# A hybrid decoder layer on one core: the head's norm weights spread by TensorE, x loaded ahead of the weights, first weight tiles in row halves

## The chip, the cores and the metric

The kernel runs on one core of one Trainium2 chip. The metric is the device time of one execution in microseconds (us). The profile shown is of one execution; start times in it count from the start of its span.

## What is computed

One layer over x (256 tokens, 1024 features, fp32): half a SwiGLU FFN, a mixer (block-sparse attention beside a state-space part, one output projection), half a second FFN, and a final norm. The stretch that matters here is the start:

```python
def rms_norm(x, w):
    y = xf * lax.rsqrt(jnp.mean(xf * xf, axis=-1, keepdims=True) + EPS)
    return y * w

def swiglu(h, w1, w3, w2):
    return (jax.nn.silu(h @ w1) * (h @ w3)) @ w2

h = rms_norm(x, ffn1_norm)                     # x 256 x 1024
x = x + 0.5 * swiglu(h, ffn1_w1, ffn1_w3, ffn1_w2)   # w1, w3 1024 x 2816, w2 2816 x 1024
```

## The kernel before

Every engine's program is written out by hand in `build`, with semaphores between them; no scheduler orders anything. Tokens are in two tiles of 128 (`t` = 0, 1), features in 8 tiles of 128 (`KD`). A matrix product in fp32 is made of three products of parts in fp32r (`three`, L1099; lines 1101 to 1103): an operand is split into a high part, copied by ScalarE (`w_hi`, `hT_hi`), and a low part, the difference, made by VectorE (`w_lo`, `hT_lo`).

The first FFN takes its 22 column tiles of w1 and w3 in 11 steps of two (`odd` = 0, 1). Step 0 is laid out by tokens: `pair_product(n, t, odd)` (L1148) multiplies the transposed, normed tile `t` with tile `odd` of w1 and w3 together, 8 feature tiles by three matmuls of 256 columns. From step 1 on `gate_or_up` makes the transposed result with the weights stationary.

The head, until step 1, runs as follows. The tiles are named by (odd, kind), kind 0 for w1, 1 for w3, 2 for w2.

- SP (L297 to L317) issues: x of token tile 0 in two halves, the identity (part of `cst`), the norm's weights broadcast to all 128 partitions (`norm_w`, 512 KB written), w1 and w3 of tile 0 (512 KB each), x of token tile 1, w1 and w3 of tile 1, both w2 tiles, the other constants. Then each load of step 1 (`ffn_load`, L275, 1 MB) waits until the split of the tile before it in that buffer is done (`half_ready`).
- ScalarE squares x with a sum (`square_x`, L476); POOL makes `rstd` from it (`rsqrt`, L363 and L366).
- VectorE scales x with `rstd` and the norm's weights (`scale_first`, L792), in halves of 512 features.
- TensorE multiplies the identity with itself without a use for the result (`keep_clock`, L1172; the fillers, in U_BANK), transposes the normed tile (`norm_transposes`, L1230), and ScalarE and VectorE split the transposes (`hT_hi_part`, L488; `hT_lo_part`, L813).
- ScalarE and VectorE split the weight tiles (`split_hi`, L452; `split_lo`, L770), 1024 elements per partition each.

TensorE's order is its program in `ffn`: five fillers, transposes of token tile 0, eleven fillers, product (t 0, odd 0), transposes of token tile 1, products (0, 1), (1, 0), (1, 1), then the gate product of step 1, `pair_transposes` and its up product. Each engine's instructions wait in the order in which they are written, so an instruction that waits holds all behind it.

Of the kernel before, what the change touches and what calls it, by code (L numbers as in the profile page):

```python
# [37 lines left out]
PAIR_ORDER = ((0, 0), (0, 1), (1, 0), (1, 1), (0, 2), (1, 2))  # L38
# [43 lines left out]
def build(nc, x_in, w1s, w3s, w2s, norms, w_in, conv_w, conv_b, dt_bias, A_log, D_skip,  # L82
# [4 lines left out]
    with ExitStack() as ctx:  # L87
# [29 lines left out]

        gu = sb("gu", [P, SEQ])
# [43 lines left out]
        first_loaded = [sem(f"first_loaded{k}") for k in range(3)]  # L162
        consts_loaded = sem("consts_loaded")
# [96 lines left out]

        def mix_half(m):
# [34 lines left out]
        def _(sp):  # L296
# [8 lines left out]
            sp.dma_start(norm_w[:, 0, :], norms[0].partition_broadcast(P)).then_inc(norm_loaded[0], 16)  # L305

            for odd, kind in PAIR_ORDER:
                if (odd, kind) == (1, 0):
                    load_x(1, 0)
                    load_x(1, 1)  # L310
# [35 lines left out]
        def _(pool):  # L346
# [6 lines left out]

            step(pool.memset(minus_half[:, :], -0.5))
# [44 lines left out]
            for t in range(TT):  # L399
                rsqrt(2 * t + 2, t, D)  # L400

# [45 lines left out]
        def _(act):  # L447
# [11 lines left out]
            def first_hi(kind):  # L459
                _, slot, src = ffn_half(0, 0, 0, kind)  # L460
                split_hi(slot, src, first_loaded[kind], 16, kind < 2)

# [87 lines left out]
            first_hi(0)  # L550
            norm_hi(0, 0)
            first_hi(1)
            for c in range(2):
                act.wait_ge(x_loaded[2 + c], 16)
                square_x(0, 1, c)
            ffn_hi(0, 0, 1, 0)
            ffn_hi(0, 0, 1, 1)
            norm_hi(0, 1)
# [196 lines left out]
        def _(dve):  # L755
# [29 lines left out]
            def scale_first(t):  # L785

                if t == 0:
                    dve.wait_ge(norm_loaded[0], 16)
                dve.wait_ge(rstd_ready, t + 1)
                for c, done in enumerate((scaled_left, scaled_right)):  # L790
                    cols = slice(c * 512, (c + 1) * 512)
                    dve.scalar_tensor_tensor(normed[:, t, cols], x[:, t, cols], rstd[:, t:t + 1], norm_w[:, 0, cols],  # L792
                                             ALU.mult, ALU.mult).then_inc(done, 1)

# [303 lines left out]
        def _(pe):  # L1098
# [49 lines left out]
            def pair_product(n, t, odd):  # L1148
# [26 lines left out]

# [422 lines left out]
```

## Time and profile before

| | us |
|---|---|
| median of 3 runs | 576.69 (575.89 to 576.89) |
| the profiled execution, whole | 575.76 |
| its span | 574.0 |
| TensorE matmul busy | 557.4 (97% of the span) |
| VectorE busy | 324.3 (56%) |
| ScalarE busy | 288.8 (50%) |
| POOL busy | 49.3 (9%) |

A busy time is the sum over the engine's instructions. In the rows below, PE is TensorE's matmul side, DVE VectorE, ACT ScalarE, SP the engine that issues the large loads. `128x512 x2` is an instruction form and how often it stands there; a bracket behind a row names what ended the idle time ahead of it. An fp32 matmul of the program (128x128, the fillers) shows as two rows.

### The profile page before, as it was taken

How to read it: one execution, taken by the hardware profiler on the slowest of the kernel's cores; microseconds unless marked ns; L12 is line 12 of the kernel's file. 1: busy time of each engine (PE TensorE's matmuls, PEld its weight loads, DVE VectorE, ACT ScalarE, POOL GpSimd, SP SyncE). 2: the span in 40 equal slices, each digit the busy share in tenths (PEclk: the TensorE clock that was granted, in tenths of full speed). 3: DMA queues.
4: the chain of work that ended last, by engine and by line, in shares of the span. 5: the costliest groups of instructions: out<-in, count | busy, mean ns of one | idle time of the engine just before them, and what ended most of it. 6: DMA issues, size and time to landing. Idle time of an engine off the chain costs nothing.

```text
span 574.0 us, 9569 instructions
## 1 busy us (share of the span) xinstructions
PE 557.4 (97%) x3744; PEld 511.4 (89%) x3744; DVE 324.3 (56%) x434; ACT 288.8 (50%) x463; POOL 49.3 (9%) x86
## 2 busy tenths in 40 slices
PE   5999999999999999999999999999999999999994
PEld 5999999999999979998888788789999999999993
DVE  3654554545554584877676546575545554554544
ACT  4644443444344375867666755364443444453433
POOL 1000040000000020513340102010000000000001
PEclk9999999999999999999999999999999999999998
DMA  9845497655446737556323226353566655456701
GB/s 256 313 128 200 154 288 247 219 164 188 155 157 213 242 117 210 175 175 199 113 91 113 73 75 186 107 152 121 174 215 219 193 173 165 151 196 219 219 1 74
DMA packets 69448, 98.01 MB, mean 171 GB/s; under 512 B 1828, under 2 KB 55392, under 8 KB 69424
## 3 DMA queue, kind: packets, MB, share of 16 engines
q1 hardware_dynamic: 68576, 95.21, 51.6%
q0 software_dynamic: 848, 2.47, 1.6%
q8 instruction: 16, 0.26, 0.2%
q14 instruction: 8, 0.07, 0.0%
HBM read 96.62 MB, written 1.05 MB: 170 GB/s over the span
## 4 chain that ended last, share of the span: by engine, by line
PE 92%; DVE 3%; ACT 2%; DMA 1%; POOL 1%; issue 1%; SPq 0%; POOLq 0%; DVEq 0%; ACTq 0%
PE bank L1101 28%; PE bank L1102 28%; PE bank L1103 28%; DMA raw<-in_ffn_w 1%; PE bank L1230 1%; DVE w_lo L770 1%; ACT z_silu L476 1%; PE bank L1404 1%; POOL mean_sq L363 1%; DVE x L782 1%; PE bank L1403 1%; PE bank L1375 1%; PE bank L1376 1%; PE bank L1362 1%; PE bank L1374 0%
## 5 line engine op out<-in xcount | busy, mean ns | idle before, releaser
L770 DVE TENSOR_TENSOR w_lo<-raw,w_hi 128x1024 fp32r<-128x1024 f32 x176 | 211.1, 1228 | 148.0 <-ACT w_hi L452 147.3
L452 ACT ACTIVATE w_hi<-raw 128x1024 fp32r<-128x1024 f32 x176 | 179.6, 1054 | 112.3 <-PE bank L1103 70.7
L1101 PE MATMUL bank<-hT_hi,w_hi 128*128 128x256 f32 x736 | 208.6, 283 | 0.0
L1103 PE MATMUL bank<-hT_hi,w_lo 128*128 128x256 f32 x736 | 208.3, 283 | 0.0
L1102 PE MATMUL bank<-hT_lo,w_hi 128*128 128x256 f32 x736 | 208.2, 283 | 0.0
L1101 PEld LDWEIGHTS bank<-hT_hi,w_hi 128*128 128x128 f32 x736 | 141.1, 192 | 1.6
L1102 PEld LDWEIGHTS bank<-hT_lo,w_hi 128*128 128x128 f32 x736 | 141.1, 192 | 1.4
L1103 PEld LDWEIGHTS bank<-hT_hi,w_lo 128*128 128x128 f32 x736 | 141.1, 192 | 0.0
L1101 PE MATMUL bank<-w_hi,hT_hi 128*128 128x512 f32 (+1 forms) x192 | 69.6, 362 | 0.6 <-DVE w_lo L770 0.5
L1101 PE MATMUL bank<-w_hi,gu_hi 128*128 128x512 f32 x176 | 69.2, 393 | 0.3
L1102 PE MATMUL bank<-w_lo,gu_hi 128*128 128x512 f32 x176 | 69.0, 392 | 0.0
L1103 PE MATMUL bank<-w_hi,gu_lo 128*128 128x512 f32 x176 | 68.5, 389 | 0.0
L1103 PE MATMUL bank<-w_hi,hT_lo 128*128 128x512 f32 (+1 forms) x192 | 68.2, 355 | 0.0
L1102 PE MATMUL bank<-w_lo,hT_hi 128*128 128x512 f32 (+1 forms) x192 | 68.0, 354 | 0.0
L503 ACT ACTIVATE gu_hi<-gu 128x256 fp32r<-128x256 f32 x40 | 16.7, 419 | 88.8 <-DVE gu L827 83.1
L1101 PEld LDWEIGHTS bank<-w_hi,hT_hi 128*128 128x128 f32 x192 | 36.3, 189 | 5.7 <-DVE w_lo L770 1.3
L1103 PEld LDWEIGHTS bank<-w_hi,hT_lo 128*128 128x128 f32 x192 | 36.3, 189 | 5.3
L1102 PEld LDWEIGHTS bank<-w_lo,hT_hi 128*128 128x128 f32 x192 | 36.4, 189 | 4.3
L1103 PEld LDWEIGHTS bank<-w_hi,gu_lo 128*128 128x128 f32 x176 | 33.1, 188 | 7.2
L1101 PEld LDWEIGHTS bank<-w_hi,gu_hi 128*128 128x128 f32 x176 | 33.2, 189 | 6.9 <-issue 1.1
L1102 PEld LDWEIGHTS bank<-w_lo,gu_hi 128*128 128x128 f32 x176 | 33.2, 189 | 5.3
L363 POOL TENSOR_SCALAR mean_sq<-sumsq 128x1 f32<-128x1 f32 x8 | 4.8, 594 | 346.2 <-ACT z_silu L476 346.2
(164 smaller groups left out, 423.2 us busy)
## 6 DMA issues: line engine op xcount, KB each, us to landing
raw<-in_ffn_w SPq DMA_DIRECT2D x63, 1024.0 KB, 5.5
raw<-in_w_in SPq DMA_DIRECT2D x16, 1024.0 KB, 5.5
raw<-in_w_out SPq DMA_DIRECT2D x6, 1024.0 KB, 4.9
raw<-in_ffn_w SPq DMA_DIRECT2D x6, 512.0 KB, 7.2
x<-in_x SPq DMA_DIRECT2D x4, 256.0 KB, 4.1
out_x<-normed SPq DMA_DIRECT2D x4, 256.0 KB, 2.1
norm_w<-in_ffn_norm SPq DMA_DIRECT2D x1, 512.0 KB, 5.5
norm_w<-in_mix_norm POOLq DMA_DIRECT2D x1, 512.0 KB, 6.6
```

The costliest lines, as they stand in the source:

```text
L363: step(pool.tensor_scalar(m, sumsq[:, 0, col:col + 1], sumsq[:, 1, col:col + 1], EPS, ALU.add, ALU.add))
L452: act.activation(by_tile(dst) if columns else dst, src, ACT.Copy).then_inc(hi_ready, 1)
L476: act.activation(z_silu[:, t, cols], x[:, t, cols], ACT.Square, scale=D ** -0.5, accum_out=sumsq[:, c, r:r + 1]).then_inc(sq_ready, 1)
L503: act.activation(gu_hi[:, odd, :], gu[:, :], ACT.Copy).then_inc(gu_hi_ready, 1)
L770: dve.tensor_tensor(lo, src, hi, ALU.subtract).then_inc(half_ready, 1)
L782: dve.scalar_tensor_tensor(xs, bank[:, 2 * t + c, :], 1.0 if n == 2 else 0.5, xs, ALU.mult, ALU.add).then_inc(x_ready, 1)
L1101: pe.matmul(dst, lhs[0], rhs[0], start=start, stop=False, skip_group_check=True)
L1102: pe.matmul(dst, lhs[0], rhs[1], start=False, stop=False, skip_group_check=True)
L1103: return pe.matmul(dst, lhs[1], rhs[0], start=False, stop=stop, skip_group_check=True)
L1230: last = pe.transpose(bank[:, bank_n, k * P:(k + 1) * P], normed[:, t, col + k * P:col + (k + 1) * P], ident)
L1362: pe.matmul(b[:, 0:384], select_r[:, h:h + 1].to_broadcast([P, P]), csT[:, :], start=True, stop=False, skip_group_check=True)
L1375: pe.matmul(bank[:, 7, o], m[:, P:SEQ], x_tok[:, 0, c], start=True, stop=False)
```

## The change

- The norm's weights come as one row of 1024 numbers (4 KB) into partition 0. TensorE spreads it over the partitions by two fp32 products with a row of ones (`spread_norm`), each of 512 columns, into two PSUM banks, at the very start of its program. `scale_first` reads the weights from there. POOL sets the row of ones first.
- SP loads all of x behind that row, and only then weights. The first tiles of w1 and w3 come in halves of four feature tiles, 256 KB each: both upper halves, then both lower.
- ScalarE squares all of x first; then it takes hT_hi's halves and the upper weight halves in turn, the lower halves, hT_hi of token tile 1, and the second pair of weight tiles behind it. VectorE takes hT_lo and the upper halves in turn, scales token tile 1, and splits w3's lower half; POOL splits w1's lower half.
- TensorE: five fillers in place of eleven ahead of the first product, which now waits for the upper halves alone, and again at feature tile 4 for the lower ones. In the first FFN product (1, 0) comes before product (0, 1).

```diff
@@ SP
             sp.dma_start(cst[:, C_ID:C_ID + P], consts[:, C_ID:C_ID + P]).then_inc(ident_loaded, 16)
-            sp.dma_start(norm_w[:, 0, :], norms[0].partition_broadcast(P)).then_inc(norm_loaded[0], 16)
-
-            for odd, kind in PAIR_ORDER:
-                if (odd, kind) == (1, 0):
-                    load_x(1, 0)
-                    load_x(1, 1)
+            sp.dma_start(norm_row, norms[0].rearrange("(a d) -> a d", a=1)).then_inc(norm_loaded[0], 16)
+            load_x(1, 0)
+            load_x(1, 1)
+            for low in range(2):
+                for kind in range(2):
+                    src = (w1s, w3s)[kind][0].rearrange("(k p) f -> p k f", p=P)[:, 4 * low:4 * low + 4, 0:P]
+                    sp.dma_start(first_src(kind, low), src).then_inc((first_loaded if low else first_top_loaded)[kind], 16)
+            for odd, kind in SECOND_ORDER:
@@ POOL
+            pool.memset(ones_row, 1.0).then_inc(ones_ready, 1)
...
             for t in range(TT):
                 rsqrt(2 * t + 2, t, D)
+            _, slot, _ = ffn_half(0, 0, 0, 0)
+            pool.wait_ge(hi_ready, 1)
+            pool.tensor_tensor(first_part(w_lo[:, slot, :], 1), first_src(0, 1),
+                               first_part(w_hi[:, slot, :].bitcast(f32), 1), ALU.subtract).then_inc(first_low_ready, 1)
@@ ScalarE
+            def first_rows_hi(kind, low):
+                act.wait_ge((first_loaded if low else first_top_loaded)[kind], 16)
+                act.activation(first_part(w_hi[:, ffn_half(0, 0, 0, kind)[1], :], low), first_src(kind, low),
+                               ACT.Copy).then_inc(hi_ready if low else first_top_hi, 1)
...
                 square_x(0, 0, c)
-            first_hi(0)
-            norm_hi(0, 0)
-            first_hi(1)
             for c in range(2):
                 act.wait_ge(x_loaded[2 + c], 16)
                 square_x(0, 1, c)
+            hT_hi_part(hT_count(0) + 1, T_BANKS[0], 0, 0)
+            first_rows_hi(0, 0)
+            hT_hi_part(hT_count(0) + 2, T_BANKS[1], 4, 0)
+            first_rows_hi(1, 0)
+            first_rows_hi(0, 1)
+            first_rows_hi(1, 1)
+            norm_hi(0, 1)
             ffn_hi(0, 0, 1, 0)
             ffn_hi(0, 0, 1, 1)
-            norm_hi(0, 1)
             first_hi(2)
@@ VectorE
-                if t == 0:
-                    dve.wait_ge(norm_loaded[0], 16)
                 dve.wait_ge(rstd_ready, t + 1)
                 for c, done in enumerate((scaled_left, scaled_right)):
+                    if t == 0:
+                        dve.wait_ge(norm_spread, c + 1)
                     cols = slice(c * 512, (c + 1) * 512)
-                    dve.scalar_tensor_tensor(normed[:, t, cols], x[:, t, cols], rstd[:, t:t + 1], norm_w[:, 0, cols],
+                    dve.scalar_tensor_tensor(normed[:, t, cols], x[:, t, cols], rstd[:, t:t + 1], bank[:, 2 + c, :],
                                              ALU.mult, ALU.mult).then_inc(done, 1)
...
             scale_first(0)
-            ffn_lo(0, 0, 0, 0)
-            norm_lo(0, 0)
+            hT_lo_part(hT_count(0) + 1, T_BANKS[0], 0, 0)
+            first_rows_lo(0, 0).then_inc(first_top_ready, 1)
+            hT_lo_part(hT_count(0) + 2, T_BANKS[1], 4, 0)
+            first_rows_lo(1, 0).then_inc(first_top_ready, 1)
             for c in range(2):
                 dve.wait_ge(x_loaded[2 + c], 16)
-            ffn_lo(0, 0, 0, 1)
             scale_first(1)
+            dve.wait_ge(first_low_ready, 1)
+            first_rows_lo(1, 1).then_inc(half_ready, 2)
+            norm_lo(0, 1)
             ffn_lo(0, 0, 1, 0)
             ffn_lo(0, 0, 1, 1)
-            norm_lo(0, 1)
@@ TensorE
                     if odd == 0 and k % 4 == 0:
                         pe.wait_ge(hT_ready, hT_count(2 * n) + 2 * t + k // 4 + 1)
+                    if n + t + odd == 0 and k == 4:
+                        pe.wait_ge(half_ready, 2)
...
                 if n == 0:
                     norm_transposes(0, 0)
-                    keep_clock(11)
-                h0 = FFN_HALF0[n]
-                pe.wait_ge(half_ready, h0 + 2)
+                    keep_clock(5)
+                    pe.wait_ge(first_top_ready, 2)
+                else:
+                    pe.wait_ge(half_ready, h0 + 2)
                 pair_product(n, 0, 0)
                 norm_transposes(2 * n, 1)
+                if n == 0:
+                    pair_product(n, 1, 0).then_inc(pair_used, 1)
                 pe.wait_ge(half_ready, h0 + 4)
                 pair_product(n, 0, 1).then_inc(pair_done, 1)
-                pair_product(n, 1, 0).then_inc(pair_used, 1)
+                if n == 1:
+                    pair_product(n, 1, 0).then_inc(pair_used, 1)
                 pair_product(n, 1, 1).then_inc(pair_done, 1)
...
+            def spread_norm():
+                pe.wait_ge(ones_ready, 1)
+                pe.wait_ge(norm_loaded[0], 16)
+                for c in range(2):
+                    pe.matmul(bank[:, 2 + c, :], ones_row, norm_row[:, c * 512:(c + 1) * 512],
+                              start=True, stop=True).then_inc(norm_spread, 1)
+
+            spread_norm()
             pe.wait_ge(ident_loaded, 16)
             keep_clock(5)
             ffn(0)
```

How it moves instructions, on VectorE from the start of its program; before (`w_lo` 128x1024 is a whole weight tile, in the order (0, 0), (0, 1), then after the scaling of token tile 1 (1, 0), (1, 1)):

```order
L792 SCALAR_TENSOR_TENSOR normed<-x,rstd,norm_w 128x512 x2
L770 TENSOR_TENSOR w_lo<-raw,w_hi 128x1024
L813 TENSOR_TENSOR hT_lo<-bank,hT_hi 128x4x128 x2
L770 TENSOR_TENSOR w_lo<-raw,w_hi 128x1024
L792 SCALAR_TENSOR_TENSOR normed<-x,rstd,norm_w 128x512 x2
L770 TENSOR_TENSOR w_lo<-raw,w_hi 128x1024 x2
L813 TENSOR_TENSOR hT_lo<-bank,hT_hi 128x4x128 x2
```

and after (128x512 is half a weight tile):

```order
L825 SCALAR_TENSOR_TENSOR normed<-x,rstd,bank 128x512 x2
L852 TENSOR_TENSOR hT_lo<-bank,hT_hi 128x4x128
L831 TENSOR_TENSOR w_lo<-raw,w_hi 128x512
L852 TENSOR_TENSOR hT_lo<-bank,hT_hi 128x4x128
L831 TENSOR_TENSOR w_lo<-raw,w_hi 128x512
L825 SCALAR_TENSOR_TENSOR normed<-x,rstd,bank 128x512 x2
L831 TENSOR_TENSOR w_lo<-raw,w_hi 128x512
L852 TENSOR_TENSOR hT_lo<-bank,hT_hi 128x4x128 x2
L803 TENSOR_TENSOR w_lo<-raw,w_hi 128x1024 x4
```

The second pair of weight tiles (the first two of the last four rows' splits) stood ahead of hT_lo of token tile 1 and now stands behind it.

On ScalarE from the start of its program, after the change, with the semaphores that each waits for:

```order
L506 ACTIVATE z_silu,sumsq<-x 128x512 [waits x_loaded3]
L518 ACTIVATE hT_hi<-bank 128x4x128 [waits transposed]
L490 ACTIVATE w_hi<-raw 128x512 [waits first_top_loaded0]
L518 ACTIVATE hT_hi<-bank 128x4x128 [waits transposed]
L490 ACTIVATE w_hi<-raw 128x512 [waits first_top_loaded1]
L490 ACTIVATE w_hi<-raw 128x512 [waits first_loaded0]
L490 ACTIVATE w_hi<-raw 128x512 [waits first_loaded1]
L518 ACTIVATE hT_hi<-bank 128x4x128 [waits transposed] x2
L477 ACTIVATE w_hi<-raw 128x1024 [waits raw_loaded0]
L477 ACTIVATE w_hi<-raw 128x1024 [waits raw_loaded1]
```

Before, w1's tile stood ahead of the first hT_hi, and the two 128x1024 of the second pair ahead of hT_hi of token tile 1; now no weight tile is ahead of a transpose's split.

On TensorE from the start of its program, after the change:

```order
L1295 MATMUL bank<-norm_w,mix_w 128x512 [waits norm_loaded0,ones_ready]
L1295 MATMUL bank<-norm_w,mix_w 128x512
L1216 MATMUL bank<-cst 128x128 [waits ident_loaded]
L1216 MATMUL bank<-cst 128x128 x4
L1279 MATMUL bank<-cst,normed 128x128 [waits scaled_left]
L1279 MATMUL bank<-cst,normed 128x128 x3
L1279 MATMUL bank<-cst,normed 128x128 [waits scaled_right]
L1279 MATMUL bank<-cst,normed 128x128 x3
L1216 MATMUL bank<-cst 128x128 x5
L1143 MATMUL bank<-w_hi,hT_hi 128x256 [waits hT_ready,first_top_ready]
```

Two spreading products are new at the head, and six of the eleven fillers ahead of the first product are gone.

## Rows read from the trace of the kernel before

**Rows 1.** The page: TensorE's busy time, and the chain that ended last, by engine.

```profile
PE 557.4 (97%) x3744; PEld 511.4 (89%) x3744; DVE 324.3 (56%) x434; ACT 288.8 (50%) x463; POOL 49.3 (9%) x86
PE 92%; DVE 3%; ACT 2%; DMA 1%; POOL 1%; issue 1%; SPq 0%; POOLq 0%; DVEq 0%; ACTq 0%
```

**Rows 2.** Busy time by stretch: stretch and length, each engine (instructions), clock, DMA.

```profile
18.70:27.36 8.66, 8.64 (x72) 8.64 (x73) 5.18 (x6) 4.81 (x6) 0.00 (x0) 1.00 1.01 343
...
60.00:200.00 140.00, 139.87 (x985) 131.11 (x984) 72.08 (x84) 62.19 (x89) 6.08 (x10) 1.00 0.63 202
```

**Rows 3.** TensorE's time line, 4 to 19 us: start, length, line, operation, count.

```profile
4.52 2.50 PE L1172 MATMUL bank<-cst 128*128 128x128 f32 x10 [4.52 <-DMA cst<-in_shape_constants]
8.67 1.97 PE L1230 MATMUL bank<-cst,normed 128*128 128x128 f32 x8 [1.65 <-DVE normed L792]
10.43 4.03 PE L1172 MATMUL bank<-cst 128*128 128x128 f32 x22
14.22 0.36 PE L1101 MATMUL bank<-w_hi,hT_hi 128*128 128x256 f32 x1
...
17.17 1.03 PE L1230 MATMUL bank<-cst,normed 128*128 128x128 f32 x8
18.72 0.39 PE L1101 MATMUL bank<-w_hi,hT_hi 128*128 128x256 f32 x1 [0.52 <-DVE w_lo L770]
```

**Rows 4.** The same view, the up product of step 1.

```profile
30.69 0.36 PE L1101 MATMUL bank<-hT_hi,w_hi 128*128 128x256 f32 x1
```

**Rows 5.** VectorE's time line, the head.

```profile
7.86 1.42 DVE L792 SCALAR_TENSOR_TENSOR normed<-x,rstd,norm_w 128x512 f32<-128x512 f32 x2 [7.86 <-DMA norm_w<-in_ffn_norm]
...
11.71 1.28 DVE L813 TENSOR_TENSOR hT_lo<-bank,hT_hi 128x512 fp32r<-128x512 f32 x2
12.91 1.22 DVE L770 TENSOR_TENSOR w_lo<-raw,w_hi 128x1024 fp32r<-128x1024 f32 x1
14.98 1.42 DVE L792 SCALAR_TENSOR_TENSOR normed<-x,rstd,norm_w 128x512 f32<-128x512 f32 x2 [0.86 <-POOL rstd L366]
```

**Rows 6.** ScalarE's time line, the head.

```profile
9.48 1.06 ACT L452 ACTIVATE w_hi<-raw 128x1024 fp32r<-128x1024 f32 x1 [4.46 <-DMA raw<-in_ffn_w]
10.44 1.07 ACT L488 ACTIVATE hT_hi<-bank 128x512 fp32r<-128x512 f32 x2
...
17.80 1.09 ACT L488 ACTIVATE hT_hi<-bank 128x512 fp32r<-128x512 f32 x2 [0.53 <-PE bank L1230]
```

**Rows 7.** SP's time line: issues of the identity, the norm and step 1's w1.

```profile
1.66 0.42 SPq L304 DMA_DIRECT2D cst<-in_shape_constants  x1
2.12 0.43 SPq L305 DMA_DIRECT2D norm_w<-in_ffn_norm  x1
...
17.56 0.38 SPq L275 DMA_DIRECT2D raw<-in_ffn_w  x1
```

**Rows 8.** The page's DMA issues: count, KB each, us from issue to landing.

```profile
norm_w<-in_ffn_norm SPq DMA_DIRECT2D x1, 512.0 KB, 5.5
...
cst<-in_shape_constants SPq DMA_DIRECT2D x1, 64.0 KB, 2.8
```

**Rows 9.** The fillers (L1172) by stretch: matmuls, weight loads, clock, DMA.

```profile
10.40:13.20 2.80, 2.77 (x13) 2.80 (x14) 1.00 1.15 319
13.20:14.20 1.00, 1.00 (x10) 1.00 (x9) 1.00 1.24 305
```

**Rows 10.** POOL's time line: the first rstd.

```profile
5.59 0.57 POOL L366 TENSOR_TENSOR rstd<-mean_sq,minus_half 128x1 f32<-128x1 f32 x1
```

**Rows 11.** POOL's 512-wide operations (L426): min/median/max ns, first and last start.

```profile
L426 POOL TENSOR_TENSOR normed<-x_tok,small x4: 1042/1194/2023, 264.9 to 271.2; 128x512 f32<-128x512 f32 x4
```

**Rows 12.** Line 275, the issue at 17.56 alone (step 1's w1).

```profile
DMA to landing us min/median/max: 5.8/5.8/5.8
```

**Rows 13.** Line 275, all nine issues up to 60 us.

```profile
DMA to landing us min/median/max: 4.9/5.8/9.1
```

**Rows 14.** Line 275, the issue at 18.69 alone (step 1's w3).

```profile
DMA to landing us min/median/max: 9.1/9.1/9.1
```

More of the change, by code:

```diff
@@ L37 @@
 FT = F // P
-PAIR_ORDER = ((0, 0), (0, 1), (1, 0), (1, 1), (0, 2), (1, 2))
+SECOND_ORDER = ((1, 0), (1, 1), (0, 2), (1, 2))
 FI = FT // 2
@@ L116, in build @@
         minus_half = sb("minus_half", [P, 1])
+        norm_row = norm_w[0:1, 0, :]
+        ones_row = mix_w[0:1, D:D + P]
         gu = sb("gu", [P, SEQ])
@@ L162, in build @@
         first_loaded = [sem(f"first_loaded{k}") for k in range(3)]
+        first_top_loaded = [sem(f"first_top_loaded{k}") for k in range(2)]
+        first_top_hi = sem("first_top_hi")
+        first_top_ready = sem("first_top_ready")
+        first_low_ready = sem("first_low_ready")
+        ones_ready = sem("ones_ready")
+        norm_spread = sem("norm_spread")
         consts_loaded = sem("consts_loaded")
@@ L259, in ffn_half, with first_part, first_src @@
             return number, (FFN_HALF0[n] + slot) % HALF_SLOTS, src
+        def first_part(t, low):
+            return by_tile(t)[:, 4 * low:4 * low + 4, :]
+        def first_src(kind, low):
+            return ffn_half(0, 0, 0, kind)[2][:, 4 * low:4 * low + 4, :]
         def mix_half(m):
@@ L785, in scale_first, with first_rows_lo @@
             def scale_first(t):
-                if t == 0:
-                    dve.wait_ge(norm_loaded[0], 16)
                 dve.wait_ge(rstd_ready, t + 1)
                 for c, done in enumerate((scaled_left, scaled_right)):
+                    if t == 0:
+                        dve.wait_ge(norm_spread, c + 1)
                     cols = slice(c * 512, (c + 1) * 512)
-                    dve.scalar_tensor_tensor(normed[:, t, cols], x[:, t, cols], rstd[:, t:t + 1], norm_w[:, 0, cols],
+                    dve.scalar_tensor_tensor(normed[:, t, cols], x[:, t, cols], rstd[:, t:t + 1], bank[:, 2 + c, :],
                                              ALU.mult, ALU.mult).then_inc(done, 1)
+            def first_rows_lo(kind, low):
+                slot = ffn_half(0, 0, 0, kind)[1]
+                dve.wait_ge(*((hi_ready, kind + 1) if low else (first_top_hi, kind + 1)))
+                return dve.tensor_tensor(first_part(w_lo[:, slot, :], low), first_src(kind, low),
+                                         first_part(w_hi[:, slot, :].bitcast(f32), low), ALU.subtract)
             def weigh_x(n, t, c):
@@ L1174, in ffn @@
             def ffn(n):
+                h0 = FFN_HALF0[n]
                 if n == 0:
                     norm_transposes(0, 0)
-                    keep_clock(11)
-                h0 = FFN_HALF0[n]
-                pe.wait_ge(half_ready, h0 + 2)
+                    keep_clock(5)
+                    pe.wait_ge(first_top_ready, 2)
+                else:
+                    pe.wait_ge(half_ready, h0 + 2)
                 pair_product(n, 0, 0)
                 norm_transposes(2 * n, 1)
+                if n == 0:
+                    pair_product(n, 1, 0).then_inc(pair_used, 1)
                 pe.wait_ge(half_ready, h0 + 4)
                 pair_product(n, 0, 1).then_inc(pair_done, 1)
-                pair_product(n, 1, 0).then_inc(pair_used, 1)
+                if n == 1:
+                    pair_product(n, 1, 0).then_inc(pair_used, 1)
                 pair_product(n, 1, 1).then_inc(pair_done, 1)
```

## The prediction

> **What bounds the kernel now.** I read the engines and the chain that ended last first [rows 1]: TensorE's matmul side is busy 97% of the span and holds 92% of the chain. Then the stretches [rows 2]: from 60 to 200 us it is busy 139.87 of 140 us. So a microsecond won or lost before the first ordinary FFN step reaches the end unshortened, and one that does not move TensorE's queue there is worth nothing. The change touches only the first 30 us, so the question is when TensorE starts the gate product of step 1 (24 matmuls after the four first products), and then the up product behind it.
>
> TensorE's own time line of the head [rows 3] gives the milestones: filler 4.52 to 7.02, first transposes at 8.67, filler from 10.43, first product at 14.22, transposes of the second token tile at 17.17, then at 18.72 three products and the gate without a gap. The three take 72 matmuls in 8.64 us [rows 2], 0.12 each or 2.88 a product, so the gate starts at 18.72 + 8.64 = 27.36. After it come the pair transposes, and the up product at 30.69 [rows 4], 3.33 after the gate. The 1.5 us between the transposes and 18.72 hold 0.5 us of waiting for the split of the second weights.
>
> Next, what the first product at 14.22 waited for. VectorE [rows 5]: the scaling starts at 7.86, when the broadcast norm weights land, and the last weight split starts at 12.91 and ends at 14.13. ScalarE [rows 6]: w1's tile at 9.48, when it has landed, hT_hi at 10.44, w3's tile behind them.
>
> **The queues.** Today's norm load writes 512 KB and lands 5.5 us after its issue at 2.12, thus at 7.6, 3.2 us behind the identity (issued 1.66, 2.8 us: 4.46) [rows 7, 8]. A 4 KB row in its place lets everything behind it land an estimated 3 us earlier: x all by about 6, the w1 and w3 rows by about 10, the second pair by about 13. SP's issues stay as many plus two. None of this is on the path after the change, as follows, so I cost it at nothing; the cover is ScalarE's queue, which comes to those tiles only after the transposes.
>
> **TensorE up to the transposes.** The row lands behind the identity, at 4.5 to 4.9; I take 4.6. TensorE then spreads it: two fp32 products of 512 columns. No such product is in the trace. The nearest rows are the filler's, 128 columns in two rows each: 13 rows in 2.80 us up to 13.2, ten in 1.00 after it [rows 9]. That is 0.215 us a row, then half: 1.2 and then 2.4 GHz (the granted clock in these rows reads 1.00 in both, so I go by the durations). Eight rows' worth is 1.72 us slow or 0.86 fast; I take slow, because the filler's first stretch (10 rows in 2.50 us from 4.5) was slow throughout. Spreading: 4.6 + 3.44 = 8.04. Behind it stand the five fillers, then the transposes. The clock rose at 13.2 after 4.6 us of unbroken work since 8.67; the same from 4.6 on gives 9.2. Ten filler rows from 8.04: five and a half slow until 9.2, the rest fast, 0.5 us, so 9.7. The scaling is done by then: rstd at 6.16 [rows 10], left half from 6.2, right half after 8.04 plus 0.75, 8.95 with its start. So **the transposes start at T = 9.7, a microsecond later than now (8.67)**, behind work that the change itself added.
>
> The Trainium skill (page TensorE: Matmul & The Clock Gate, Part 4: PE-mode transpose) says that transposes do not count as work that raises the clock. By that rule the rise at 13.2 came 2.8 us after the filler's start at 10.43, and spreading would reach the fast level sooner; the first rival prices that. This trace can't tell: the first fillers stayed slow to their end, and the second turned fast with transposes and fillers both ahead of the rise.
>
> **From T to the first product.** All durations from [rows 3, 5, 6]; 512-wide operations start 0.48 apart on ScalarE (two hT_hi in 1.07) and 0.60 apart on VectorE (two hT_lo in 1.28, 0.68 each). ScalarE starts hT_hi 0.63 after the transposes (17.17 to 17.80). Then ScalarE: hT_hi at T+0.63, w1 top 1.11, hT_hi 1.59, w3 top 2.07, w1 low 2.55, w3 low 3.03 to 3.62. VectorE: hT_lo at T+1.25, w1 top 1.85, hT_lo 2.45, w3 top 3.05 to 3.73. **First product at T+3.79 = 13.5, against 14.22: 0.7 us won.** Of the eleven fillers six go; the five that stay end near T+2, ahead of that wait, so their loss costs and gains nothing unless the clock falls in the 1.8 us between, which it did not in the 1.5 us after 17.2.
>
> **Then the waits that are new.** VectorE goes on to the second tile's scaling (two in 1.42): T+3.65 to 5.07; then w3 low 4.99 to 5.67. POOL does w1 low from T+3.14; its only 512-wide operations take 1.04 to 2.02 us [rows 11], so T+4.2 to 5.2, hidden or 0.2 over. The first product's lower half waits for both: its upper half ends at T+3.79+1.44 = 5.23, it goes on at 5.73 and ends at **7.17** (0.5 us idle). Transposes of the second tile from 7.20, 0.86 long. Now the second product is that tile's own, so nothing covers its conversion: hT_hi at 7.83 to 8.42, hT_lo 8.45 to 9.13, product from **9.19** (1.1 us idle) to 12.07. Queued behind that conversion on ScalarE and VectorE stand the second pair's splits, landed long before: ScalarE 8.79 to 10.8, VectorE 9.88 to 11.1 and 11.02 to 12.25. The third product starts at 12.31 (0.2 idle), and two end at **T+18.07 = 27.8**, 0.4 us later than now.
>
> **The next load.** SP issues step 1's w1 when the split at T+11.1 ends, at 20.85; today at 17.56 [rows 7], covered by 9.8 us of queued products. It landed after 5.8 us [rows 12]; the nine loads of its size up to 60 us take 4.9 to 9.1 [rows 13]. I take 5.8, the same load: 26.65. ScalarE 1.06, VectorE 1.22 and the hand-overs make 2.4: the gate starts at 29.05, after 1.2 us of waiting, **1.7 us later than 27.36**. W3 is issued at 9.7+12.3 = 22.0; today's took 9.1 [rows 14], partly behind transfers that are gone. With that it lands at 31.1 and the up product starts at 33.5, 2.8 late; a megabyte at the 343 GB/s of [rows 2] takes 3.1, so at best it is ready at 26.65+3.1+2.4 = 32.2, before gate and transposes (3.33 us) end at 32.4, 1.7 late. Between the two, nearer the shorter since its queue is emptier: 0.4 us of further wait. **Sum: 2.1 us slower.** Against the profiled execution's 575.76 us that makes 577.9; the median of the runs shown is 0.93 above it, so I forecast **578.8**.
>
> **Rivals.** *The clock rises early*: slow rows from 4.6 only until 7.4, like the 2.8 us of fillers before 13.2; it is what the page's rule would make of this head. Spreading ends at 7.75, the filler at 8.85, T is 0.85 us earlier and the sum +1.25: 577.9. For: thirteen filler rows stood before the rise. Against: the stretch 4.5 to 7.0 stayed slow. If the load also takes 4.9 us, the gate starts at 27.3 as today, and the up product up to 0.3 late: 577.0.
> *Faster*: everything at the fast level from 4.6, T = 4.6+1.72+1.08 = 7.4, and w1 landing in 4.9: gate at 7.4+11.15+4.9+2.4 = 25.85, 1.5 us early, 575.2. It decides from T below 8.0 at a 5.8 us load. Against: no row before 13.2 is fast.
> *A slow load*: step 1's w1 takes 9.1 us like w3 today: gate at 32.35, 5.0 late, 581.7. For: the second load of the head takes that long. Against: it stood behind others.
> *The row is no cheaper*: it lands at 7.6 as the broadcast did, T at 12.7, 5.1 late, 581.8. Against: 4 KB against 512.
> *Slow until past the transposes*: T 10.2, hT_hi 0.5 us later, 3.1 us slower: 579.8, inside my range.
>
> **How the numbers follow.** Forecast with its bounds on clock and loads (+0.8 to +3.6) 0.60; early clock 0.22; slow load 0.06; slow row 0.03; faster 0.06; no difference, by some error of the sum, 0.03. A measurement of this kernel tells about 0.2%, 1.15 us, from no change. A tenth of the forecast and half of the early clock lie within that. So faster 0.06, within 0.20, slower 0.74. The range leaves out the slow cases and the fast one: 576.7 to 580.8.
>
> **What would show it.** Right: transposes at 9 to 10 us behind 128x512 rows; first product near 13.5 with a gap at its middle; about 1 us of TensorE waiting for hT_lo ahead of the second; the gate waiting for w_lo, behind a DMA issued near 21. Wrong: transposes before 8.7, or the gate starting at 27 or earlier.

## The result: slower by 0.3%, and the profile after

| | before | changed |
|---|---|---|
| median, us (8 runs each) | 576.57 (575.89 to 576.95) | 578.06 (577.96 to 580.21) |
| ratio, 95% interval | | 1.003 (1.0021 to 1.004) |
| the profiled execution, us | 575.76 | 577.97 |
| its span, us | 574.0 | 576.1 |
| first transposes | 8.67 | 10.19 |
| first product | 14.22 | 14.46 |
| gate of step 1 | 27.36 | 29.73 |
| up product of step 1 | 30.69 | 33.06 |

The forecast was 578.8, and slower. The medians differ by 1.49 us and the profiled executions by 2.21; the kernel before was profiled in an execution quicker than all eight of its runs here. The up product of step 1 starts 2.37 us later. What comes behind it takes the same in both: 575.76 - 30.69 = 545.07 before, 577.97 - 33.06 = 544.91 after.

The page of the changed kernel, its first and its chain section: TensorE is as busy, and holds about the same share of the chain, as in [rows 1].

```profile
PE 558.9 (97%) x3736; PEld 510.0 (89%) x3736; DVE 324.2 (56%) x435; ACT 289.0 (50%) x465; POOL 50.6 (9%) x88
PE 91%; DVE 3%; ACT 2%; DMA 1%; POOL 1%; issue 1%; SPq 0%; POOLq 0%; DVEq 0%; ACTq 0%
```

TensorE's time line of the changed kernel, the head; it answers to [rows 3] and [rows 4]. L1295 are the spreading products (a fp32 product is two rows), L1216 the fillers, L1279 the transposes, L1143 the first matmul of a product:

```profile
4.21 3.75 PE L1295 MATMUL bank<-norm_w,mix_w 1*128 1x512 f32 x4 [4.21 <-DMA norm_w<-in_ffn_norm]
7.89 2.50 PE L1216 MATMUL bank<-cst 128*128 128x128 f32 x10
10.19 1.71 PE L1279 MATMUL bank<-cst,normed 128*128 128x128 f32 x8
...
14.46 0.39 PE L1143 MATMUL bank<-w_hi,hT_hi 128*128 128x256 f32 x1 [1.45 <-DVE w_lo L831]
...
16.49 0.36 PE L1143 MATMUL bank<-w_hi,hT_hi 128*128 128x256 f32 x1 [0.34 <-DVE w_lo L831]
...
20.01 0.38 PE L1143 MATMUL bank<-w_hi,hT_hi 128*128 128x256 f32 x1 [0.98 <-DVE hT_lo L852]
...
23.11 0.39 PE L1143 MATMUL bank<-w_hi,hT_hi 128*128 128x256 f32 x1
...
29.73 0.39 PE L1143 MATMUL bank<-hT_hi,w_hi 128*128 128x256 f32 x1 [0.60 <-DVE w_lo L803]
...
33.06 0.36 PE L1143 MATMUL bank<-hT_hi,w_hi 128*128 128x256 f32 x1
```

Three things stand in these rows. The norm's row lands at 4.21 (its broadcast held VectorE until 7.86 in [rows 5]). Then come six microseconds of spreading and fillers ahead of the transposes. After them the first product waits 1.45 us for the splits, where before the fillers ran up to it. Behind its start come the four new waits: inside the first product, ahead of the second (token tile 1), ahead of the third, and ahead of the gate. The third has no bracket: it starts 3.10 us behind the second's start, where a product takes 2.88.

VectorE and ScalarE of the changed kernel, their time lines; [rows 5] and [rows 6] are the same before:

```profile
11.91 0.69 DVE L852 TENSOR_TENSOR hT_lo<-bank,hT_hi 128x512 fp32r<-128x512 f32 x1 [3.17 <-ACT hT_hi L518]
12.52 0.68 DVE L831 TENSOR_TENSOR w_lo<-raw,w_hi 128x512 fp32r<-128x512 f32 x1
13.12 0.68 DVE L852 TENSOR_TENSOR hT_lo<-bank,hT_hi 128x512 fp32r<-128x512 f32 x1
13.72 0.68 DVE L831 TENSOR_TENSOR w_lo<-raw,w_hi 128x512 fp32r<-128x512 f32 x1
14.32 1.40 DVE L825 SCALAR_TENSOR_TENSOR normed<-x,rstd,bank 128x512 f32<-128x512 f32 x2
15.65 0.69 DVE L831 TENSOR_TENSOR w_lo<-raw,w_hi 128x512 fp32r<-128x512 f32 x1
19.26 1.29 DVE L852 TENSOR_TENSOR hT_lo<-bank,hT_hi 128x512 fp32r<-128x512 f32 x2 [2.92 <-ACT hT_hi L518]
20.69 4.63 DVE L803 TENSOR_TENSOR w_lo<-raw,w_hi 128x1024 fp32r<-128x1024 f32 x4
```

```profile
11.28 0.60 ACT L518 ACTIVATE hT_hi<-bank 128x512 fp32r<-128x512 f32 x1 [3.62 <-PE bank L1279]
...
18.63 1.08 ACT L518 ACTIVATE hT_hi<-bank 128x512 fp32r<-128x512 f32 x2 [4.19 <-PE bank L1279]
19.60 3.90 ACT L477 ACTIVATE w_hi<-raw 128x1024 fp32r<-128x1024 f32 x4
...
27.36 1.06 ACT L477 ACTIVATE w_hi<-raw 128x1024 fp32r<-128x1024 f32 x1 [0.68 <-DMA raw<-in_ffn_w]
```

Both engines stand idle, ScalarE 4.19 us and VectorE 2.92 us, ahead of hT of token tile 1, with the second pair of weight tiles queued behind it: it is split from 19.60 and 20.69, where before ScalarE took it at 14.45 and 16.21. So step 1's w1 is issued at 21.95 in place of 17.56 [rows 7]; it lands 5.3 us after its issue. Line 291, that issue alone:

```profile
21.95 0.38 SPq L291 DMA_DIRECT2D raw<-in_ffn_w  x1
```

```profile
DMA to landing us min/median/max: 5.3/5.3/5.3
```

### The profile page after: what moved, and what is told of

Its sections match the earlier page's. It is cut to its first block, busy times and chain, and to the rows that moved or that the text cites. A ratio compares the mean times of both kernels' runs of the same rounds, so it can differ in the third digit from the quotient of the medians.

```text
span 576.1 us, 9563 instructions
## 1 busy us (share of the span) xinstructions
PE 558.9 (97%) x3736; PEld 510.0 (89%) x3736; DVE 324.2 (56%) x435; ACT 289.0 (50%) x465; POOL 50.6 (9%) x88
## 4 chain that ended last, share of the span: by engine, by line
PE 91%; DVE 3%; ACT 2%; DMA 1%; POOL 1%; issue 1%; SPq 0%; POOLq 0%; DVEq 0%; ACTq 0%
PE bank L1143 28%; PE bank L1144 27%; PE bank L1145 27%; PE bank L1279 1%; DMA raw<-in_ffn_w 1%; DVE w_lo L803 1%; PE bank L1295 1%; PE bank L1216 1%; PE bank L1462 1%; DVE x L815 1%; PE bank L1461 1%; PE bank L1433 1%; PE bank L1434 1%; ACT z_silu L506 1%; PE bank L1420 1%
## 5 line engine op out<-in xcount | busy, mean ns | idle before, releaser
L803 DVE TENSOR_TENSOR w_lo<-raw,w_hi 128x1024 fp32r<-128x1024 f32 x174 | 208.6, 1228 | 145.2 <-ACT w_hi L477 144.4
L477 ACT ACTIVATE w_hi<-raw 128x1024 fp32r<-128x1024 f32 x174 | 177.3, 1054 | 104.6 <-PE bank L1145 69.6
L1143 PE MATMUL bank<-hT_hi,w_hi 128*128 128x256 f32 x736 | 208.7, 284 | 0.6 <-DVE w_lo L803 0.6
L1143 PEld LDWEIGHTS bank<-hT_hi,w_hi 128*128 128x128 f32 x736 | 141.1, 192 | 2.4 <-DVE w_lo L803 0.8
L1143 PE MATMUL bank<-w_hi,hT_hi 128*128 128x512 f32 (+1 forms) x192 | 69.7, 363 | 2.8 <-DVE w_lo L831 1.8
L1143 PE MATMUL bank<-w_hi,gu_hi 128*128 128x512 f32 x176 | 69.2, 393 | 0.3
L1143 PEld LDWEIGHTS bank<-w_hi,hT_hi 128*128 128x128 f32 x192 | 36.3, 189 | 8.5 <-DVE w_lo L831 1.6
L1143 PEld LDWEIGHTS bank<-w_hi,gu_hi 128*128 128x128 f32 x176 | 33.2, 189 | 6.8 <-issue 1.1
```

Source lines behind the costliest of these rows:

```text
L477: act.activation(by_tile(dst) if columns else dst, src, ACT.Copy).then_inc(hi_ready, 1)
L803: dve.tensor_tensor(lo, src, hi, ALU.subtract).then_inc(half_ready, 1)
L1143: pe.matmul(dst, lhs[0], rhs[0], start=start, stop=False, skip_group_check=True)
```

## The experiments

Theory: TensorE's queue bounds the head, and the change lengthens it in two places, by slow spreading and fillers ahead of the transposes and by the new order behind the first product. Rivals: the order is neutral and the start carries all; the loads set the gate anyway; the row is the gain and the rest the loss. The start of the up product serves as the measure in each profile: in all fourteen executions profiled, the time less that start is between 544.88 and 545.15 us. So the rows up to about 35 us explain each profiled execution, and nothing behind them differs by more than 0.3 us.

| kernel | row lands | first product | gate | up product | median, us | ratio to before (95%) |
|---|---|---|---|---|---|---|
| before | | 14.22 | 27.36 | 30.69 | 576.57 | |
| changed | 4.21 | 14.46 | 29.73 | 33.06 | 578.06 | 1.003 (1.0021 to 1.004) |
| e1_order | 4.21 | 14.39 | 27.35 | 30.66 | 575.60 | 0.9991 (0.9982 to 1.0) |
| e2_nofill | 4.11 | 12.11 | 27.63 | 31.97 | 576.83 | 1.002 (1.001 to 1.003) |
| e3_warm | 4.56 or earlier | 14.67 | 30.11 | 33.45 | 578.39 | 1.0048 (1.0035 to 1.0061) |
| e5_splits | 5.43 | 15.67 | 29.86 | 33.23 | 577.15 | 1.0018 (1.0009 to 1.0027) |
| e4_order_nofill | 4.17 | 12.17 | 25.38 | 28.70 | 573.73 | 0.9956 (0.9943 to 0.9969) |
| e6_full | 5.99 | 16.23 | 31.53 | 35.10 | 577.82 | 1.0017 (1.0001 to 1.0033) |
| e7_order_full_nofill | 5.10 or earlier | 13.13 | 26.11 | 29.41 | 574.38 | 0.9958 (0.9945 to 0.9971) |
| e9_row_only | 4.26 | 15.13 | 28.40 | 31.74 | 576.92 | 1.0009 (1.0 to 1.0018) |
| e11_row_nofill | 5.27 | 14.56 | 27.24 | 30.58 | 575.50 | 0.9981 (0.9972 to 0.999) |
| e13_best_ones12 | 6.60 or earlier | 12.61 | 25.56 | 28.88 | 573.96 | 0.9963 (0.9951 to 0.9975) |
| e10_ones8 (one run) | 5.86 | 13.62 | 29.15 | 32.48 | 577.42 | |
| e12_ones16 (one run) | 6.53 or earlier | 13.47 | 28.74 | 32.07 | 576.95 | |

"Row lands" is the start of the spreading, where it waited for the row. Where three products follow without a gap the gate is their start plus 8.64 us, as in the prediction. Ratios compare with runs of the kernel before on the same chip (medians there 576.21 to 576.59). A start is of the one execution that was profiled, a median of all; where the executions of a kernel scatter, the text says so.

### The order alone: e1_order

```diff
@@ TensorE, both FFNs in the old order
-                if n == 0:
-                    pair_product(n, 1, 0).then_inc(pair_used, 1)
                 pe.wait_ge(half_ready, h0 + 4)
                 pair_product(n, 0, 1).then_inc(pair_done, 1)
-                if n == 1:
-                    pair_product(n, 1, 0).then_inc(pair_used, 1)
+                pair_product(n, 1, 0).then_inc(pair_used, 1)
@@ ScalarE (VectorE the same with _lo)
-            norm_hi(0, 1)
             ffn_hi(0, 0, 1, 0)
             ffn_hi(0, 0, 1, 1)
+            norm_hi(0, 1)
```

> The changed kernel with the old order after the first product: TensorE takes product (0, 1) second, and ScalarE and VectorE split the second pair of weight tiles ahead of hT of token tile 1. Theory (the new order costs 2.3 us at the gate: 1.25 us wait for hT_lo, 0.3 us for the second pair, 0.9 us for step 1's load, issued at 21.95 in place of about 17.5): first product at 14.5 as in the changed kernel, gate at about 27.4, as before the change; total about 576.5, that is 1.5 to 2.3 us under the changed kernel. Rival (the slow clock and the spreading at the start carry the loss, the order is neutral): gate stays at 29.7, total 578.0.

Measured: the first product at 14.39, and from 18.71 three products and the gate without a gap, TensorE's time line:

```profile
17.92 1.04 PE L1276 MATMUL bank<-cst,normed 128*128 128x128 f32 x8
18.71 0.36 PE L1143 MATMUL bank<-w_hi,hT_hi 128*128 128x256 f32 x1
```

The up product starts 2.40 us earlier than in the changed kernel, and the median is 2.46 lower. The order is what made the change a loss: with the other parts kept, the gate is where it was before the change. The rival of the neutral order falls. Against the kernel before the ratio is 0.9991, 0.8 us by the medians on that chip, though the gates of the two profiles are equal, because the profile of before is of a quick execution.

### Splits first, TensorE's order kept: e5_splits

The second half of e1_order's edit without the first.

> The changed kernel, TensorE's order untouched, but ScalarE and VectorE split the second pair ahead of hT of token tile 1. Theory: the second product still starts at about 20.0 behind hT_lo, the third and the gate wait for nothing, since the second pair is split by 18.7 and step 1's w1 is issued at about 17.5; gate at 20.0 + 8.64 = 28.65, 1.1 us under the changed kernel: 576.9. Rival (the load has its length whatever its issue, the gate waits for it still): 578.0.

Measured: in this profile the row landed 1.22 us later than in the changed kernel's (5.43), so lengths are compared from the first product on. From there to the gate it takes 29.86 - 15.67 = 14.19 us against 15.27: 1.08 less, as expected, and neither the third product nor the gate waits. What is left against e1_order (12.96) is 1.23, for the wait for hT_lo ahead of the second product. The median fell by 0.9 us; the expected gate of 28.65 was missed by the late row alone. Seven of the eleven executions took 576.76 to 577.16, close to the 576.9 expected, and the profiled one 578.14.

### Fewer fillers: e2_nofill, and with the order: e4_order_nofill

```diff
             spread_norm()
             pe.wait_ge(ident_loaded, 16)
-            keep_clock(5)
             ffn(0)
```

> The changed kernel without the five fillers between the spreading and the first transposes. Theory (TensorE's own queue sets the first transposes): they start at 7.9 to 8.0, the second half at 8.8, 1.4 us less for everything behind, the gate at 28.0 to 28.6, total 576.5 to 577.0. Rival 1 (the fillers bring the clock up, without them more work behind is slow): the first product starts 1.4 us earlier but runs slow in part, gate as in the changed kernel, 578.0. Rival 2 (step 1's load sets the gate, whatever goes before): 578.0 with a longer wait for it.

Measured: the transposes start at 7.79 in place of 10.19 and the first product at 12.11, 2.35 us earlier. Only 1.09 of it reaches the up product, which now waits for w_lo, since step 1's w3 took 8.9 us to land:

```profile
31.97 0.39 PE L1143 MATMUL bank<-hT_hi,w_hi 128*128 128x256 f32 x1 [0.77 <-DVE w_lo L803]
```

The gate came at 27.63, 2.10 us earlier, after 0.87 us of waiting for its split, so the second rival (578.0, the load sets the gate) falls; but the loads of step 1 take back the rest once TensorE is early enough in the changed order. The total of 576.83 lies in the theory's 576.5 to 577.0, though not in its way: the gain at the gate was larger than forecast, and a microsecond of it was given back behind it. The first rival falls too: the first product ran fast from its second row on.

> Old order of the products and splits (as in e1_order) and no fillers between the spreading and the transposes (as in e2_nofill). Theory (the two losses lie one behind the other in TensorE's queue and add up): first product near 12.1, product (0, 1) near 16.6, held by the split of w3's second tile, which lands near 14.2; gate near 25.2; 2.1 us under e1_order, about 573.5. Rival (the clock: without the fillers the rise comes too late and the rest of the head runs slow): gate at 27, no gain on e1_order, 575.6.

Measured: 573.73 us, 0.44% under the kernel before and 1.9 under e1_order. TensorE's time line, its last row from the weight-load side (PEld):

```profile
4.17 3.75 PE L1292 MATMUL bank<-norm_w,mix_w 1*128 1x512 f32 x4 [4.17 <-DMA norm_w<-in_ffn_norm]
7.84 2.03 PE L1276 MATMUL bank<-cst,normed 128*128 128x128 f32 x8
...
12.17 0.54 PE L1143 MATMUL bank<-w_hi,hT_hi 128*128 128x256 f32 x1 [0.17 <-DVE w_lo L831]
...
16.74 0.39 PE L1143 MATMUL bank<-w_hi,hT_hi 128*128 128x256 f32 x1
...
16.73 0.19 PEld L1143 LDWEIGHTS bank<-w_hi,hT_hi 128*128 128x128 f32 x1 [0.24 <-DVE w_lo L803]
```

The matmul row at 16.74 has no bracket, but the weight load with it waited 0.24 us for w3's split, and the product starts 1.03 us behind its transposes, against 0.79 in e1_order. ScalarE took the tile at 14.36, when it had landed, and VectorE's split ended at 16.68. So the second product is held by that split, by 0.24 us, as the theory had it. With the old order step 1's loads are early again. This is the lowest median of the study; e7_order_full_nofill and e13_best_ones12 below have ratios within its interval.

### The row alone: e9_row_only, and without fillers: e11_row_nofill

Both start from the kernel before: the row's load, the ones, `spread_norm` and the scaling from PSUM, and nothing else of the change; e11 also drops the `keep_clock(5)` ahead of the transposes.

> The kernel before with one part of the change: the norm's weights as a row that TensorE spreads; whole first tiles, order of loads, products, splits and eleven fillers as before. Theory (the row halves and x ahead of the weights bring little: the conversions of hT come last on VectorE in either form): transposes at 10.2, first product at 14.5 to 14.8, gate at 27.4 to 27.8, total within 0.5 us of the kernel before. Rival (the row is the gain and the rest the loss): the first product at 13 or earlier, total 1 us or more under the kernel before.

Measured: transposes at 10.22, first product at 15.13, gate at 28.40. The product came 0.3 us later than the theory's bound and the gate 0.6, but the total is within 0.5 us of the kernel before and the rival falls: the row alone gains nothing, since six microseconds of TensorE's work stand behind it.

> e9_row_only (the kernel before, with the norm row that TensorE spreads as its one part of the change) without the five fillers ahead of the transposes: whole first tiles, old orders everywhere, eleven fillers behind the transposes. Against e4_order_nofill it lacks the row halves and x ahead of the weights. Theory (the row and the missing fillers carry the gain, the halves little): transposes at 7.9, first product at 12.3 to 13.0, product (0, 1) at 17.4, gate at 26.1, total 574.0 to 575.0. Rival (the halves are worth as much as the fillers): gate at 27 or later, 576.

Measured: gate at 27.24, where the rival had it, and a median of 575.50, 1.4 us under e9 but 0.5 over the theory's bound. The eleven executions fall into two groups: five at 574.60 to 574.96, inside the theory's range, and six at 575.50 to 575.68, with the profiled one among them. Its time line:

```profile
5.27 3.75 PE L1249 MATMUL bank<-norm_w,mix_w 1*128 1x512 f32 x4 [5.27 <-DMA norm_w<-in_ffn_norm]
8.95 2.03 PE L1235 MATMUL bank<-cst,normed 128*128 128x128 f32 x8
10.77 4.04 PE L1177 MATMUL bank<-cst 128*128 128x128 f32 x22
14.56 0.36 PE L1106 MATMUL bank<-w_hi,hT_hi 128*128 128x256 f32 x1
```

The row landed at 5.27, 1.10 us later than in e4_order_nofill, and the eleven fillers behind the transposes, most of them slow, hold TensorE to the moment of the first product. Behind it the second product waits for the split of the second pair in both kernels, 0.62 us in e9 and 0.3 in e11, since VectorE comes to that pair only after a scaling of token tile 1 that waited 0.96 us for `rstd`; with all of x squared first, as in the change, that wait is not there. Of the 1.86 us between this gate and that of e4_order_nofill 1.10 are thus the late row, and 0.76 are the eleven fillers, the halves and the early x together. No run takes the halves or the early x without the row, so what each is worth by itself stays open.

### What raises the clock: e3_warm, e6_full, e10_ones8, e12_ones16

Each puts extra products ahead of the spreading of the changed kernel, without a use for their results. The edit of e3_warm:

```diff
                 pe.wait_ge(ones_ready, 1)
+                for _ in range(8):
+                    pe.matmul(bank[:, U_BANK, 0:P], ones_row, ones_row, start=True, stop=True)
                 pe.wait_ge(norm_loaded[0], 16)
```

In e3 both operands are the row of ones (one partition), in e6 two 128x128 tiles of zeros (`cs_rows`), in e10 and e12 two of ones (`gu`, set by POOL). There are eight such products, and sixteen in e12.

> The changed kernel with eight more products of the ones row with itself (one partition, 128 columns) ahead of the spreading, from about 1 us on, while the norm row is still on its way. Theory (the spreading is slow since nothing ran before, and any product raises the clock): the spreading runs at the fast level in part or whole, its four rows take 1.9 to 2.8 us in place of 3.4, the transposes start 1.5 to 3 us earlier (7.2 to 8.7), total 575.2 to 576.6. Rival (one-row products do not raise it): all rows up to 11.4 us stay slow and the total stays 578.0.

Busy time by stretch of e3_warm; the first column behind the length is TensorE's matmul side with its rows:

```profile
0.90:4.50 3.60, 3.52 (x16) 3.52 (x17) 0.00 (x0) 1.99 (x4) 0.47 (x4) 1.00 0.61 193
4.50:8.10 3.60, 3.60 (x6) 1.05 (x4) 0.75 (x1) 1.54 (x5) 0.87 (x2) 1.00 0.92 265
8.10:13.90 5.80, 5.80 (x28) 5.80 (x28) 2.52 (x4) 2.88 (x7) 0.88 (x2) 1.00 1.11 304
```

TensorE had work without a break from 0.98 on, and each of the rows to 13.9 is slow: 28 rows in 5.8 us are 0.21 each, against 0.11 fast. (The granted clock reads 1.00 there as well; it tells the level only behind the first rise, so the lengths of the rows decide.) The theory fails and the rival holds: one-row products did not raise the clock, neither these nor the spreading. All six executions took 578.31 or more.

> The changed kernel with eight products of 128 rows by 128 columns from about 1.4 us on, ahead of the spreading, on a tile of zeros, in place of e3_warm's products of one row. Theory (it is work on the full array that raises the clock, and products of one partition do not count): the clock rises 3 to 6 us after their start, at 4.5 to 7.2, the spreading and the five fillers run at the fast level in part, transposes at 7.5 to 9.3, total 575.7 to 577.2. Rival (the clock rises only some time into the kernel, or needs other data than zeros): rise at 11 or later as before, total 578.1 to 578.4.

In the profiled execution zeros did not either, though they fill the array: all rows of e6_full up to 13.8 are slow, the spreading took 3.7 us again, and the row landed late besides:

```profile
1.39 3.78 PE L1294 MATMUL bank<-cs_rows 128*128 128x128 f32 x16 [1.39 <-POOL cs_rows L374]
5.99 3.74 PE L1298 MATMUL bank<-norm_w,mix_w 1*128 1x512 f32 x4 [0.82 <-DMA norm_w<-in_ffn_norm]
```

But that execution, 580.07, is the slowest of twelve, and the twelve fall into two groups: six at 579.01 to 580.07, and six at 575.87 to 576.63. The zeros hold the spreading to 5.10 or later (it starts there in e7_order_full_nofill), so with slow rows the transposes start at 11.1, 0.9 us behind the changed kernel's: an estimated 578.9, which is where the slow group begins. The quick group is 3 us shorter and lies where the theory put an early rise (575.7 to 577.2). No execution of it was profiled. So the rival holds for the profiled execution, and whether zeros raised the clock in the others stays open.

e7_order_full_nofill is e4_order_nofill with the same eight products of zeros. It was expected to start the first product at 10.5 to 11.5 and still have the gate near 25.2, since the second product would wait for w3's split; its rival was a further 1 to 2 us under e4. Measured: every row ahead of the first product is slow, the zeros held the spreading to 5.10, and the first product started at 13.13, the gate at 26.11, with a median of 574.38 (573.42 to 574.65). TensorE was later by 0.7 us at the gate in place of earlier, so neither theory nor rival was put to the test.

> e6_full with a tile of ones in place of the tile of zeros. Theory (zeros are no work for what raises the clock): the clock rises at 4.5 to 8, the transposes start by 9. Rival (zeros were not the cause: the work on the full array was too short before the one-row products came): rise at 11 or later, as with zeros.

> e10_ones8 with sixteen such products, 6.9 us of unbroken work on the full array from 1.4 us on if all slow. Theory (unbroken work on the full array raises the clock after 3.1 to 5.8 us, as in the six kernels profiled so far): it rises between 4.5 and 7.2, within these products. Rival (it can't rise before some 11 us of the kernel): rise at 11 or later although the work began at 1.4.

With ones in the tile the clock was up when the spreading began, in both; each is a single execution. Stretches of e10_ones8: its eight products, the spreading, the fillers' first part, the rest with the first transposes.

```profile
1.30:5.00 3.70, 3.70 (x16) 3.42 (x16) 0.00 (x0) 2.16 (x5) 0.38 (x2) 1.00 0.69 201
5.70:7.70 2.00, 1.84 (x4) 0.66 (x4) 0.57 (x1) 0.82 (x3) 0.40 (x1) 1.00 1.06 340
7.70:8.70 1.00, 1.00 (x8) 0.94 (x8) 0.92 (x2) 0.62 (x2) 0.28 (x1) 0.94 1.18 314
8.70:11.00 2.30, 2.30 (x12) 2.30 (x12) 0.00 (x0) 0.55 (x2) 0.59 (x2) 0.50 1.14 289
```

The spreading's four rows take 1.98 us in place of 3.75. Then the granted clock falls to 0.50, from 2.4 to 1.2 GHz: after 0.84 us of waiting for the row and the one-row spreading it is slow again for most of the fillers and the transposes, which start at 9.35 (by 9 expected). In e12_ones16, whose full products end directly before the spreading, 32 rows take 5.37 us, the spreading 1.98, and the clock stays:

```profile
1.23 5.37 PE L1295 MATMUL bank<-gu 128*128 128x128 f32 x32 [1.23 <-POOL gu L373]
6.53 1.98 PE L1298 MATMUL bank<-norm_w,mix_w 1*128 1x512 f32 x4
```

The rows turn fast at about 4.5, inside the products, so the rival (no rise before some 11 us) falls. Yet the up product comes only 1.0 us earlier than in the changed kernel: sixteen products delay the spreading to 6.53, and behind the first product the changed order's waits are untouched. Eight zeros against eight ones is one execution against one, so the data as the cause is not shown.

### Both together: e13_best_ones12

e4_order_nofill with twelve full products of ones ahead of the spreading.

> e4_order_nofill with twelve products of a tile of ones (128 rows) ahead of the spreading, so that the clock rises near 5 and spreading, transposes and fillers run at the fast level. Theory (in e4_order_nofill the second product pair waits for nothing but its own tiles: w3's second tile lands near 14.3 and is split by 16.7): transposes at 6.9 to 7.2, first product near 11, but product (0, 1) at 16.5 and the gate at 25.1 as in e4_order_nofill; total within 0.5 us of its 573.7. Rival (TensorE's queue still bounds the head): gate near 24.3 and total 572.7 or less.

Measured: gate at 25.56, 573.96 us, the same as e4_order_nofill, which the theory expected, but not by the early start that it counted on. The twelve products held the spreading to 6.60, so the transposes started at 8.77 (7.84 in e4_order_nofill). They ran fast, but the granted clock fell at about 9.9, so the fillers behind them were slow again and the first product started at 12.61 (12.17 there):

```profile
10.00:13.00 3.00, 2.66 (x13) 2.36 (x13) 2.94 (x5) 2.82 (x7) 0.86 (x1) 0.50 1.17 301
```

ScalarE took w3's second tile at 14.53, when it had landed, and its split ended at 16.84; the transposes ended at 16.92, where the second product started. So a faster TensorE would have gained at most 0.1 us there before that split held it, as it does in e4_order_nofill.

## Why the prediction was right, and where it was not

**The path: right.** What moved the total is TensorE's queue up to step 1, and what the loads behind the norm gained reached nothing in the changed kernel. That gain was put at 3 us; for the second pair of weight tiles it was 1.8 (ScalarE waited for them until 12.65 and 14.36 in e4_order_nofill, until 14.45 and 16.21 before).

**TensorE up to the transposes: mis-sized.** The row landed at 4.21 (4.6 assumed), and the fillers followed the spreading 3.68 us later (3.44 assumed; the rows start 0.85 to 0.99 apart). The step that failed is "The clock rose at 13.2 after 4.6 us of unbroken work since 8.67; the same from 4.6 on gives 9.2". It rose at about 11.5, ahead of the last two of the eight transposes: TensorE's matmul side by stretch in the changed kernel, 18 rows in 3.60 us, then 13 in 1.40.

```profile
7.90:11.50 3.60, 3.60 (x18) 1.00 1.12 297
11.50:12.90 1.40, 1.40 (x13) 1.00 1.20 306
```

The spreading did not bring the rise forward, and in e3_warm 7.1 us of such rows did not either. Besides, the moment of the rise scatters: the changed kernel, e1_order and e9_row_only run the same kinds of rows up to 10.2, and turn fast at 11.5, 11.0 and 13.4. So T was 10.19, not 9.7, and the transposes were slow: hT_hi came 1.09 behind them, not 0.63. The first product started at 14.46 where 13.5 was forecast: 0.24 us lost, not 0.7 won. That is the rival "slow until past the transposes" (T 10.2, 3.1 us slower), here with a quicker load.

**Transposes and the clock.** The early-clock rival fell, and by the one-row products: both it and the forecast took the spreading for work like the fillers, and no term of either allowed for a difference. In the changed kernel and in e1_order the clock rose while the transposes ran, with 2.3 us of fillers ahead of them, so they don't hinder a rise; whether they help one can't be told. The rule of the Trainium skill that the prediction cites (page TensorE: Matmul & The Clock Gate, Part 4: PE-mode transpose), that transposes do not count as work for the clock, is thus decided by no run here.

**The new waits: right in place and size.** From the first product: second product after 5.40 forecast, 5.55 measured; third 8.52 and 8.65; gate 15.55 and 15.27. The wait inside the first product was 0.34 us (0.5 forecast), that for hT_lo 0.98 (1.1). POOL's half split took 1.56 us, inside the 1.04 to 2.02 assumed, and cost nothing.

**The next load: right in kind.** Issued at T+11.1 = 20.85 forecast, 21.95 measured (0.5 of it by T, 0.5 by slow transposes), landed after 5.3 in place of 5.8. The further 0.4 us for the up product was nil: it starts 3.33 behind the gate as before. In e2_nofill that wait is there (0.77).

**The sum**: 2.1 us forecast against 2.37 at the up product and 2.21 between the profiled executions. That is closer than the terms deserve, and luck: the first product was put 0.96 us too early, and what follows 0.7 too long (0.28 from there to the gate, 0.4 for the up product). By medians the loss is 1.5, within the range. The kernel before scatters over 1 us, its profiled execution was a quick one, and the changed kernel's was an ordinary one; so the 0.93 added to reach the first median made the forecast 0.7 too high. What makes the kernel before scatter was not looked into.

## What to carry to other kernels

When two products share an engine, try the one whose operand is converted last in the last place. Here, swapping it forward left three engines waiting and delayed the reuse of a buffer, and so the issue of the next load, by 4.5 us (21.95 against 17.44 in e1_order). A load that lands earlier gains nothing if the engine that uses it stands behind a new wait; read the queue of each engine, not the landing. And work put ahead of the first useful instruction is paid in full there, at the slow clock: dropping the five fillers gained 1.9 us where the order was right. Last, look at the list of all executions before a profile is taken for the kernel: that of e6_full is the slowest of two unlike groups.

## What the runs showed of the hardware

- Products that use one partition did not raise TensorE's clock in 7.1 us of unbroken work (e3_warm, 0.98 to 8.10). A spreading of such products after a rise was followed by a fall in e10_ones8 (at about 8.6) and e13_best_ones12 (at about 9.9), and by none in e12_ones16.
- Eight products of ones on the full array left the clock up for the spreading behind them (e10_ones8, one execution); eight of zeros did not in the profiled executions of e6_full and e7_order_full_nofill. Six of e6_full's twelve executions are 3 us shorter than the rest, so it is not shown that zeros can't.
- The moment of the rise scatters: 11.0 to 13.4 us in three kernels whose TensorE rows are alike up to 10.2 (e1_order, changed, e9_row_only).
- The granted clock in a stretch's row reads 1.00 before the first rise, though the rows take twice as long there.
- A load of a single 4 KB row, issued at 2.1, landed at 4.1 to 4.3 us in five profiled kernels and 5.3 to 6.0 in four, with the same issues ahead of it. Where TensorE waits for it at its first instruction, a late row delays all behind it (e5_splits, 1.22 us). In the changed kernel it landed ahead of the 64 KB identity, which was issued before it (1.65) and took 3.9 us; the prediction had it behind.
